# Two passes over a weight slab become one, with the split of weights one slab further ahead

## The reference, cut to what matters

```
z = u @ w_in[i]                      # 2048 wide input, up to 7176 columns
h = h + mixed @ w_o[i]
h = h + (p[i] @ w_ple[i]) * sigmoid(h @ w_pg[i])
...
u, z = split(h @ w_in, 2); o = (mixed * silu(z)) @ w_out
x = x + gate * o
```

## Time and profile before

| what | value |
|---|---|
| runs | 3160.41, 3144.35, 3154.27 us; median 3154.27 |
| profiled execution, first to last instruction | 3147.7 us (6.6 us under the median of the runs) |
| mean granted TensorE clock | 0.973 |
| TensorE matmuls busy | 94% of the span |
| VectorE busy | 81% |
| ScalarE busy | 45% |
| DMA | 705.62 MB moved, 224 GB/s |

### The profile page before, as it was taken

The page is one execution under the profiler, slowest core; times in us unless marked ns, Lnnn a source line. Parts: engine busy times, 40 slices in busy tenths (PEclk is TensorE's granted clock), DMA queues, the critical chain, the costliest instruction groups (busy, mean ns, idle before and its releaser), DMA issues.

```text
span 3147.7 us, 46326 instructions
## 1 busy us (share of the span) xinstructions
PE 2943.2 (94%) x17906; PEld 2558.8 (81%) x17906; DVE 2564.6 (81%) x3622; ACT 1406.0 (45%) x1560; POOL 273.0 (9%) x530
## 2 busy tenths in 40 slices
PE   5999999989999999999999897998898999899998
PEld 4887888868888888888888787886687788778887
DVE  7988789987889889979876887787878986687586
ACT  4434563544445535544343344344734334434443
POOL 0000000000000000000001110101010422010000
PEclk9999999989999999999999998998998999999999
DMA  5775347757654577666777775875275665376563
GB/s 221 287 254 209 139 171 274 265 195 268 235 202 172 183 286 254 223 212 247 268 268 254 281 273 178 295 261 176 75 264 207 229 214 193 136 282 228 209 239 141
DMA packets 130914, 705.62 MB, mean 224 GB/s; under 512 B 16392, under 2 KB 16544, under 8 KB 72608
## 3 DMA queue, kind: packets, MB, share of 16 engines
q1 hardware_dynamic: 67392, 480.28, 42.6%
q0 software_dynamic: 61264, 214.93, 19.4%
q10 hardware_dynamic: 2064, 7.70, 0.7%
HBM read 696.07 MB, written 2.10 MB: 222 GB/s over the span
## 4 chain that ended last, share of the span: by engine, by line
PE 69%; DVE 17%; DMA 5%; issue 5%; ACT 4%; ACTq 0%; DVEq 0%; POOLq 0%
PE pair L639 34%; PE pair L626 21%; DMA aslab<-w_ada_dram 5%; DVE wlo L1900 4%; DVE aslab L1925 3%; ACT whi L1222 2%; PE pair L622 1%; PE pair L623 1%; DVE sc L2139 1%; PE bank L1000 1%; DVE junk L1925 1%; PE pair L700 1%; PE bank L1115 1%; PE bank L781 1%; DVE u L2150 1%
## 5 line engine op out<-in xcount | busy, mean ns | idle before, releaser
L639 PE MATMUL pair<-u,whi 128*128 128x512 f32 x6016 | 1483.8, 400 | 82.8 <-DVE u L2197 17.4
L639 PEld LDWEIGHTS pair<-u,whi 128*128 128x128 f32 x6016 | 1131.4, 192 | 324.2 <-issue 58.1
L1222 ACT CAST whi<-raw 128x2048 fp32r<-128x2048 f32 x456 | 863.9, 1896 | 898.1 <-PE pair L626 860.2
L1900 DVE TENSOR_TENSOR wlo<-raw,whi 128x2048 fp32r<-128x2048 f32 x456 | 1034.3, 2269 | 275.3 <-ACT whi L1222 273.9
L626 PEld LDWEIGHTS pair<-u,wlo 128*128 128x128 f32 x6656 | 859.7, 193 | 53.9 <-DVE wlo L1900 22.5
L626 PE MATMUL pair<-u,wlo 128*128 128x256 f32 x6656 | 880.5, 285 | 18.1 <-DVE wlo L1900 18.0
L566 POOL DMA_DIRECT2D aslab<-w_ada_dram x384 | 202.9, 528 | 2628.4 <-DVE mod L1925 1354.1
L1925 DVE CUSTOM_DVE_ANT_0 aslab<-aslab,sil,part 128x1024 f32<-128x1024 f32 x192 | 244.9, 1280 | 58.5 <-DMA aslab<-w_ada_dram 58.4
L1925 DVE CUSTOM_DVE_ANT_0 aslab<-aslab,sil,cols 128x1024 f32<-128x1024 f32 x192 | 244.9, 1280 | 43.5 <-DMA aslab<-w_ada_dram 43.4
L622 PE MATMUL pair<-u,whi 128*128 128x256 f32 x640 | 162.4, 292 | 7.8 <-ACT whi L1222 4.6
L623 PE MATMUL pair<-u,whi 128*128 128x256 f32 x640 | 158.8, 286 | 0.0
(11 more groups left out here) (310 smaller groups left out, 2567.8 us busy)
## 6 DMA issues: line engine op xcount, KB each, us to landing
aslab<-w_ada_dram POOLq DMA_DIRECT2D x384, 512.0 KB, 4.9
raw<-w_wfi_dram SPq DMA_DIRECT2D x96, 1024.0 KB, 5.0
raw<-w_win_dram SPq DMA_DIRECT2D x56, 1024.0 KB, 4.9
raw<-w_wfo_dram SPq DMA_DIRECT2D x48, 1024.0 KB, 5.3
raw<-w_wci_dram SPq DMA_DIRECT2D x48, 1024.0 KB, 5.1
raw<-w_wga_dram SPq DMA_DIRECT2D x32, 1024.0 KB, 4.8
raw<-w_wo_dram SPq DMA_DIRECT2D x32, 1024.0 KB, 5.7
raw<-w_wpg_dram SPq DMA_DIRECT2D x32, 1024.0 KB, 4.9
```

Of the source, the lines that this page charges most:

```text
L639: last = nc.tensor.matmul(two(o[:, :]), whi[:, s % 2, wc], both_u[:, :, kt, :], start=kt == 0, stop=False, skip_group_check=True)
L1222: nc.scalar.copy(whi[:, s % 2, 0:n], raw[:, s, 0:n]).then_inc(s_hi, 1)
L1900: v.tensor_tensor(wlo[:, s, 0:n], raw[:, s, 0:n], whi[:, s % 2, 0:n].bitcast(F32), ALU.subtract).then_inc(s_lo, 1)
```

## The change

- `slab_t` takes one pass: for each weight tile the wide matmul with whi and right behind it the narrow one with wlo. PE waits for `s_lo` of the slab before it begins. The other kinds keep two passes.
- `whi` has three places (`WHI`). Slab m is split when slab m-3 has been multiplied. At the start of the kernel one slab more is split, and from there each call, now `split_next`, takes the next slab in order: at every place of the programs it is the slab behind the one that was split there before.
- The buffers begin at 8320 bytes and not at 16512, which makes room for the third place.
- The hardware loops of PE in `in0` and `in1` are written out.
- `ple` slabs, of 1024 columns, get halves of the three places.

```diff
+WHI = 3
+DMA_RING = 8192
+SLAB_AT = [(r, g, s) for r in RUNS for g in range(r["n"]) for s in range(SLABS)]
-        base = 16512
+        base = DMA_RING + 128
-        whi_t = sb("whi", 2 * 2048, F32R)
+        whi_t = sb("whi", WHI * 2048, F32R)
+        def whi_of(r, g, s):
+
+            m = SLABS * (r["m0"] + g) + s
+            if r["kind"] != "E":
+                return whi[:, m % WHI, 0:r["width"]]
+            return whi[:, m % WHI, 1024 * (s // WHI):1024 * (s // WHI) + 1024]
-            def slab_t(s, par, lows, ready=None, kb=0):
+            def slab_t(wh, s, par, ready=None, kb=0):
...
-                        if lows:
-                            last = low(o[:, 0:T], wlo[:, s, wc], uhi[:, kt, :], kt == KT - 1)
-                        else:
-                            last = nc.tensor.matmul(two(o[:, :]), whi[:, s % 2, wc], both_u[:, :, kt, :],
-                                                    start=kt == 0, stop=False, skip_group_check=True)
+                        nc.tensor.matmul(two(o[:, :]), wh[:, wc], both_u[:, :, kt, :],
+                                         start=kt == 0, stop=False, skip_group_check=True)
+                        last = low(o[:, 0:T], wlo[:, s, wc], uhi[:, kt, :], kt == KT - 1)
...
-                        pe.wait_ge(s_hi, (g + r["m0"]) * SLABS + (s + 1))
-                        slab(s, par, False, ready, kb)
+                        pe.wait_ge(s_lo, (g + r["m0"]) * SLABS + (s + 1))
+                        last = slab(wh, s, par, ready, kb)
...
+            ahead = iter(enumerate(SLAB_AT))
+
+            def split_next():
+
+                m, (r, g, s) = next(ahead, (None, (None, None, None)))
+                if m is None:
+                    return
+                act.wait_ge(s_raw[s], (m // SLABS + 1) * 16)
+                before = m - WHI if r["kind"] != "E" or s < WHI else m - 2 * WHI
+                if before >= 0:
+                    act.wait_ge(s_slab, before + 1)
+                nc.scalar.copy(whi_of(r, g, s), raw[:, s, 0:r["width"]]).then_inc(s_hi, 1)
...
             def first_block(l):
                 if l == 0:
-                    split(RUN["in0"], 0, 0)
+                    split_next()
                 norm(f"n{l}")
+                if l == 0:
+                    split_next()
```

More of the change, by code:

```diff
@@ L664, in slab_h, with slab_kv @@
                         else:
[L665 removed]
+                            last = high(o, wh[:, wc], uhi[:, kt, :], ulo[:, kt, :], kt == 0 and b == 0)
                 return last
[L668 removed]
+            def slab_kv(wh, s, par, lows):
                 for k in range(4):
@@ L684, in slab_kv, with slab_n @@
                         else:
-                            nc.tensor.matmul(o, uhi[:, kt, tk], whi[:, s % 2, wc], start=kt == 0 and t == 0,
+                            nc.tensor.matmul(o, uhi[:, kt, tk], wh[:, wc], start=kt == 0 and t == 0,
                                              stop=False, skip_group_check=True)
-                            last = low(o, ulo[:, kt, tk], whi[:, s % 2, wc], False)
+                            last = low(o, ulo[:, kt, tk], wh[:, wc], False)
                 return last
-            def slab_n(s, par, lows, width):
+            def slab_n(wh, s, par, lows, width):
                 for k in range(4):
@@ L699, in slab_n @@
                         else:
-                            nc.tensor.matmul(o, uhi[:, kt, tk], whi[:, s % 2, wc], start=kt == 0,
+                            nc.tensor.matmul(o, uhi[:, kt, tk], wh[:, wc], start=kt == 0,
                                              stop=False, skip_group_check=True)
-                            last = low(o, ulo[:, kt, tk], whi[:, s % 2, wc], False)
+                            last = low(o, ulo[:, kt, tk], wh[:, wc], False)
                 return last
@@ L729, in group @@
                         pe.wait_ge(s_hi, (g + r["m0"]) * SLABS + (s + 1))
[L730 to L734, removed]
+                        slab(wh, s, par, False)
+                        if middle is not None:
+                            middle(s)
+                        pe.wait_ge(s_lo, (g + r["m0"]) * SLABS + (s + 1))
+                        last = slab(wh, s, par, True)
                     last.then_inc(s_slab, 1)
@@ L750, in one @@
                     group(r, g, slab, fill if g == g0 else None, behind if sums else None)
[L751 to L755, removed]
-                            for odd in range(2):
-                                group(r, j * 2 + odd, slab)
-                        g = (g0 + n) // 2 * 2
-                    else:
-                        one(g)
-                        g += 1
+                for g in range(g0, g0 + n):
+                    one(g)
             def norm(name):
```

223 lines of the change are left out of this document (96 added, 127 removed).

## The result

| | before | after |
|---|---|---|
| median of the runs | 3155.09 us | 3196.53 us |
| lowest to highest | 3144.35 to 3160.41 | 3191.41 to 3204.06 |
| ratio, 95% interval | | 1.0138, 1.0114 to 1.0162 |
| profiled execution, span | 3147.7 us | 3192.1 us |
| mean granted TensorE clock | 0.973 | 0.968 |

41 us slower; the forecast was 47 us faster, and 3196 lies above the whole range.

A forecast was written before the change was run, and what follows sets the result against it. TensorE was taken as the bound, by matmul spacing and its waits. Gains of 18 (spacing) + 10 (whi) + 9 (wlo) + 9 (norms) = 46 us took the median from 3154.3 to 3108, range 3068 to 3175.

The forecast's parts named there:

- so I cost that at nothing: ACT's queue, splits one slab further ahead: a late load holds ACT by its lateness, priced at no loss.
- moves only if a load lands later than one slab time: Work queued behind ACT's wait (copies, DVE's sums, drains) shifts only for loads later than one slab, 5.57 us; median 4.9.
- the same event for ACT in the same place of its queue: ACT's wait before each split's cast was said to be unchanged by splitting one slab further ahead; no cost.
- That order is not touched.: Waits for drains, as at ao (DVE 3.08 us for an ada slab, PE 3.96), were said to stay.
- 6.9 us to spare: Low half of a slab: cast and subtraction end at 9.8 us after load issue, the slab begins at 16.7.
- (a) to (c): PE's shrinking waits: for whi 10 us gained, for wlo 9 us, for u at four norms 9 us.
- The spacing: Matmul order inside a slab: an alternating pair takes 345 ns, not 348, over 6016 pairs, 18 us gained.
- the best case: Matmul pair inside a slab: wide keeps 227 ns and narrow 113, 340 ns together, 48 us gained.
- Rival 3: DVE is the real bound, shorter waits come back at the next slab: 0 to 12 us, 3148; chance 0.10.
- Rival 4: Matmul width changes cost more than first matmuls show: pair 358 ns, 60 us lost, 3186; chance 0.12.
- rival 5: Late loads hold a quarter of 456 splits by 1.5 us: 57 us, eating the sum, 3165; chance 0.05.
- (a): PE's 9.7 us of waits for whi in 5 places, plus 1.7 us each at slow clock: 10 us gained.

The follow-up runs named there:

- one call moved: Changed kernel with the fourth ada piece of each run's first group behind the sum freeing the first bank pair, in DVE's queue: ratio 1.0096.
- the one with two passes: Changed kernel with splits still one slab further ahead but the old two passes per slab: ratio 1.0067; with the fourth ada piece behind the sum, 0.9961.
- the early wait: Splits ahead in two passes, ada piece and ple/up queue calls put right, with each slab waiting for its low half at its start: 1.0007, against 0.9923 without.
- two and two: Changed kernel with two wide matmuls, then their two narrow ones, per k tile: 1.0118; with ada piece and queue calls also put right, 0.9999, against 1.0040 by turns.
- the alternation kernel: Kernel before with one alternating pass per slab, waiting for s_lo; splits, loops and two places as before: ratio 1.0219.
- queues mended: o's first cast behind ple's first drain, up's third split behind v's last copies: changed kernel 1.0130; two passes with splits ahead and ada piece moved, 0.9923 against 0.9961.

## Why the prediction was wrong

**The step that failed first** is "so I cost that at nothing", of the splits one slab further ahead. It has two faults. That what is queued behind the cast "moves only if a load lands later than one slab time" was right, but I priced it by the median of 4.9 us in an evenly running stream. At ple the slabs are short, four in 16.3 us between the ends of slabs, 4.1 each with the 3.05 us that PE waits ahead of the first. The load of m is issued at the end of m-4, the cast may begin at the end of m-3, and 4.1 us is less than any load of a whole slab takes (4.6 us at least). ACT must stand there, and did, 6.86 us. And "the same event for ACT in the same place of its queue" forgot that the load is a second event of the same wait. At ple and up this cost some 20 us in the profile (ple 16.3 to 22.5 and 16.2 to 21.9, up 27.5 to 32.3 and 27.5 to 31.7 us, between the ends of slabs), though only 3 to 12 us in the runs that mended it.

**"That order is not touched."** I had the row that decides, an ada slab that DVE waits for ahead of a sum, and called it what stays. The order of the calls did stay, and so did the number of subtractions ahead of the sum, two; what I left out is that PE comes to the sum sooner while DVE, held by the same loads, does not. The drains went from 22.9 to 45.3 us; one call moved made the changed kernel 13 us faster, and the one with two passes 33 us. Why the fourth piece's load takes 9.4 us there (2440.85 to 2450.29) when the median of these loads is 4.9 stays open. DMA moved 279 GB/s in that window, at a share of 0.84, against 221 in the mean. Over the 384 ada loads of the changed kernel, the 34 that took over 7 us had 1.2 slab loads and 0.5 other ada loads under way beside them in the mean, the 113 under 4 us 0.5 and 0.2. So other loads are the likeliest reason, but nothing was run that takes those away.

**"6.9 us to spare"** was right late in a run and wrong in its first groups, where DVE makes u, sums and subtracts. With the calls mended, the early wait alone costs 26 us; of its 20.0 us of waits 10.2 stand in the first eight slabs of a run and the rest in the next nine. I counted gains for waits at slab starts, (a) to (c), and no price for the earlier wait.

**The spacing** was the term that was mis-sized. The pair came out at 347 or 353 ns and not at 345. The mean over those 261 slabs is 349.5, where two passes have 347.9 (5.567 / 16). Instead of 18 us gained it is some 10 us lost (1.6 ns x 6016); a run by turns against two and two gave 13. The first matmuls at a change do not tell the price in a stream of changes. The Trainium skill, page TensorE: Matmul & The Clock Gate, section Back-to-back issue gap, has loads and matmuls set the spacing together. That two orders of the same work differ, 348 and 347 or 353, agrees with it; the 340 that I drew from it for the best case was never seen.

**What was right.** The waits for whi went (9.7 to 0), those at norms fell (24.0 to 18.3), the first slab at ci ended 3 us sooner. These gains were then waited away at the next drain: at ci the end of the first slab to the end of the fifth took 27.3 us before and 32.5 after. Rival 3 named that mechanism ("come back at the next slab") with DVE's load as its cause and 3148 as its result. Rival 4 gave 3186, near the time, from a pair of 358, which was wrong; rival 5 had the loads, and 3165.

**The clock** was priced as a gain in (a), 1.7 us a place, and nowhere as a loss. A wait of 4 us and more was followed by a slab of some 8 us and not 5.7, as above; the 44 waits for the low half in the alternation kernel, 2 us each in the mean, brought its clock only from 0.973 to 0.971. Of the slabs of kind T, 14 stood behind a wait of 4 us or more, against 9 before. Those that were not interrupted again, 11 and 5, took 27 and 13 us more than calm slabs of 5.6 us: 1.8 to 2.9 each, and 2.4 behind a wait of 4.16 us as behind one of 11.37.

## What to carry to other kernels

Moving a producer one step ahead in an in-order queue is not free where it stands: list at each call what it now waits for, the load above all, and what short work for the critical engine is queued behind it. Put work that nobody needs soon, and only that, behind what frees a buffer. When a change makes one stage faster, price the next wait in the same group before counting the gain, and count a stall of TensorE of 4 us and more at its length and 2 to 3 us on top.

## What the runs showed that was not expected

- Alternating 512 and 256 column matmuls have two stable rhythms, 347 and 353 ns a pair, with the same clock and DMA share; a slab takes over the rhythm of the one before. Two and two has one, 348.3 ns a pair (5.573 us).
- The same moved call gave 33 us in one kernel and 13 in another: savings at the start of a run do not add up, in either direction (queues mended: 12 us and next to nothing).
